# Chunked sliding-window attention without 28 tensor products whose results nobody reads

## What is computed

```python
def swa_sinks(h, cos, sin, w_in, b_in, sinks, w_out, b_out):
    proj = h @ w_in + b_in
    q = apply_rope(...)   # 16 heads of 64, in 4 groups of 4
    k = apply_rope(...)   # 4 key heads
    v = proj[..., qd + kd:]
    # chunks of 64 positions; a query chunk sees its own and the previous chunk
    scores = jnp.einsum("bnqhgd,bnkhd->bnhgqk", q, kb) * (SW_HEAD_DIM ** -0.5)
    scores = jnp.where(valid, scores, -jnp.inf)
    m = jnp.maximum(jnp.max(scores, axis=-1, keepdims=True), sink)
    pexp = jnp.exp(scores - m)
    probs = pexp / (jnp.sum(pexp, axis=-1, keepdims=True) + jnp.exp(sink - m))
    o = jnp.einsum("bnhgqk,bnkhd->bnqhgd", probs, vb)
    return o.reshape(b, s, qd) @ w_out + b_out
```

## Time and profile before

| | |
|---|---|
| time, median of 3 runs | 1420.49 us (1419.34 to 1420.56) |
| profiled execution: its time | 1417.11 us |
| profiled execution: span of the trace | 1415.4 us |
| PE busy | 1360.9 us (96%) |
| DVE busy | 791.6 us (56%) |
| ACT busy | 533.4 us (38%) |
| POOL busy | 252.4 us (18%) |
| granted TensorE clock, mean | 0.993 |

### The profile page before, as it was taken

One profiled execution on the slowest core, in us unless ns is written; L12 is line 12 of the kernel. 1 busy time (PEld: TensorE's weight loads), 2 busy tenths in 40 slices (PEclk: granted clock), 3 DMA queues, 4 the chain that ended last, 5 costly groups with the idle time before them and its releaser, 6 DMA issues.

```text
span 1415.4 us, 18106 instructions
## 1 busy us (share of the span) xinstructions
PE 1360.9 (96%) x6594; PEld 1120.3 (79%) x6594; DVE 791.6 (56%) x1205; ACT 533.4 (38%) x901; POOL 252.4 (18%) x243
## 2 busy tenths in 40 slices
PE   7899999999899999999999999989999999999998
PEld 5678878888778888888888878758888888888877
DVE  5557777777674343343456677674443434435655
ACT  6444445444154132231334431453332313223344
POOL 3654545453030000000002110002010000000211
PEclk9899999999999999999999999999999999999999
DMA  6233233222323223223322352503322232223221
GB/s 176 65 84 78 60 81 84 55 61 69 99 77 117 90 91 117 89 89 102 105 89 82 97 100 66 115 6 108 116 90 89 89 119 89 89 89 104 85 80 60
DMA packets 168575, 125.67 MB, mean 89 GB/s; under 512 B 35873, under 2 KB 165186, under 8 KB 168514
## 3 DMA queue, kind: packets, MB, share of 16 engines
q1 hardware_dynamic: 167410, 123.01, 29.2%
q10 hardware_dynamic: 1104, 1.84, 0.5%
HBM read 116.96 MB, written 5.25 MB: 86 GB/s over the span
## 4 chain that ended last, share of the span: by engine, by line
PE 75%; DVE 11%; ACT 3%; issue 3%; DMA 3%; DVEq 2%; POOL 2%; POOLq 0%; SPq 0%; ACTq 0%
PE psum L148 22%; PE psum L150 21%; PE psum L149 21%; DMA xScaled<-inv_blocks 2%; PE psum L890 2%; DVE wL L140 1%; PE psum L900 1%; ACT wH L132 1%; DMA inv_blocks<-blk 1%; DVE bL L1397 1%; DVE hT L1598 1%; DVEq L1168 1%; DVE terms L1166 1%; DVE acc L1596 1%; PE psum L1917 1%
## 5 line engine op out<-in xcount | busy, mean ns | idle before, releaser
L148 PE MATMUL psum<-aH,wH 128*128 128x512 f32 x896 | 361.2, 403 | 8.3 <-issue 5.4
L150 PE MATMUL psum<-aL,wH 128*128 128x512 f32 x896 | 351.3, 392 | 0.0
L149 PE MATMUL psum<-aH,wL 128*128 128x512 f32 x896 | 350.5, 391 | 0.0
L140 DVE TENSOR_TENSOR wL<-wRaw,wH 128x2048 fp32r<-128x2048 f32 (+2 forms) x125 | 241.0, 1933 | 128.5 <-ACT wH L132 122.9
L148 PE MATMUL psum<-bH,wH 128*128 128x512 f32 x720 | 284.8, 396 | 2.3 <-DVE pleT L2043 1.6
L150 PE MATMUL psum<-bL,wH 128*128 128x512 f32 x720 | 280.9, 390 | 0.0
L149 PE MATMUL psum<-bH,wL 128*128 128x512 f32 x720 | 280.8, 390 | 0.0
L132 ACT CAST wH<-wRaw 128x2048 fp32r<-128x2048 f32 (+2 forms) x109 | 196.9, 1813 | 219.9 <-PE psum L150 219.9
L148 PEld LDWEIGHTS psum<-aH,wH 128*128 128x128 f32 x896 | 169.4, 189 | 42.0 <-issue 6.8
L150 PEld LDWEIGHTS psum<-aL,wH 128*128 128x128 f32 x896 | 169.0, 189 | 36.2
L149 PEld LDWEIGHTS psum<-aH,wL 128*128 128x128 f32 x896 | 169.6, 189 | 32.1 <-issue 0.5
(11 more groups left out here) (295 smaller groups left out, 1498.6 us busy)
## 6 DMA issues: line engine op xcount, KB each, us to landing
wRaw<-in_mlp_w_up SPq DMA_DIRECT2D x64, 512.0 KB
wRaw<-in_mlp_w_down SPq DMA_DIRECT2D x64, 512.0 KB
wRaw<-in_dn_w_in SPq DMA_DIRECT2D x32, 512.0 KB
wRaw<-in_ple_w_gate SPq DMA_DIRECT2D x16, 512.0 KB
xScaled<-inv_blocks SPq DMA_DIRECT2D x16, 256.0 KB, 3.2
wRaw<-in_sw_w_in SPq DMA_DIRECT2D x16, 256.0 KB
wRaw<-in_sw_w_out SPq DMA_DIRECT2D x16, 256.0 KB
wRaw<-in_dn_w_out SPq DMA_DIRECT2D x8, 384.0 KB
```

The source lines that it names most:

```text
L140: last = [nc.vector.tensor_tensor(o, r, h_.bitcast(F32), ALU.subtract) for o, r, h_ in zip(*([v if half is None else v[:, half * v.shape[1 ...
L148: nc.tensor.matmul(o, wh, xh, start=first, stop=False)
L149: nc.tensor.matmul(o, wl, xh, start=False, stop=False)
L150: return nc.tensor.matmul(o, wh, xl, start=False, stop=last)
```

## The change

The definition of `keep_clock` and its two calls go. Nothing else is edited; the waits of every engine, the order of all other instructions and the transfers stay as they are.

```diff
-            def keep_clock(count):
-
-                for _ in range(count):
-                    nc.tensor.matmul(bank[7], wH[:, n % 2, 0:P], X[0][:, 0, :], start=True, stop=True)
-
...
             for i in range(3):
                 scores(i, [1])
-            keep_clock(8)
             for i in range(ATB):
                 t = i // KVH
                 if i + 3 < ATB:
                     scores(i + 3, [1] if i < 1 else range(2))
-                if i < KVH:
-                    keep_clock(5)
                 pe.wait_ge(pr_ok, i + 1)
```

## The result

The changed kernel is slower: 1426.61 us median (7 runs, 1422.23 to 1429.73) against 1419.34 us for the kernel before (7 runs, the three shown above among them, 1414.87 to 1420.56), a ratio of 1.0057 with a 95% interval of 1.0038 to 1.0075. Forecast were 1418.8 us, a range up to 1421.1, and "within 0.2%". The slowdown is what rival (a) describes, to which the prediction gave 0.07.

The account below looks back on a forecast made before the run. DVE was taken to set the pace from block 4 to 15. Its waits of 0.49 + 1.39 = 1.88 us, trimmed to 1.7 for a clock fall, came off the median: 1420.49 - 1.7 = 1418.8 us, range 1416.8 to 1421.1.

Parts of the forecast that it names:

- rival (a): In the opening the clock stays at 1.2 GHz and PE becomes the bound: 4.1 us slower, 1424.6 us; chance 0.07.
- the 7.5 us on the chain: Dense products on the chain of work in the opening, 2.04 us once and 1.36 us four times; only 1.88 us gainable.
- DVE's two waits: DVE's idle time for transposes ahead of its copies of blocks 1 and 3, 0.49 and 1.39 us, would both go.
- ACT did not take over: ACT, idle 2.47 us ahead of the copy of block 2, was checked as next to be late and forecast not to be.
- The gap: Idle time of PE ahead of block 0's transposes, from 895.21 to 897.98, forecast at 2.77 us.
- a fall once, around the new gap: Clock at 1.2 GHz once near block 0's transposes, for 3.4 us; gain 1.6 to 1.88 us, or 1.1 if 6.9 us.
- the prediction's own sign of being wrong: In the opening of the changed kernel's profile, the clock being down for over 7 us would show the forecast wrong.

Follow-up runs that it names:

- the fitted kernel: Against the kernel before: dense products cut to 2, 3, 3, 3 in turns 0 to 3, four added in turn 4, eight ahead of the loop kept; ratio 0.9994.
- the first experiment: Against the kernel before: only the eight dense products ahead of the loop stay, the twenty in the first four turns go; ratio 0.9998.
- the kernel with the tail filled: The kernel before with its 28 dense products and eight more, two in turn 13 and six in turn 14; ratio 0.9993.

## Why the prediction was wrong

**What bounds the kernel, and the sum at 2.4 GHz: right.** Of the 7.5 us on the chain only DVE's two waits were to be had, 0.49 + 1.39 = 1.88 us. With the clock held in the opening (23 products, fitted to the gaps) the attention shortened by 1.85 us, the copies had no idle time ahead, and ACT did not take over.

**The gap: right.** 2.95 us against 2.77, and the clock fell around it, as said.

**The step that failed** is the one behind it: "So I expect a fall once, around the new gap, and the upper clock soon after." Its length was put at 3.4 us, or 6.9 at worst. It was 47.8 us in the profile of the changed kernel and 34.1 us in its repeat, where the prediction's own sign of being wrong was "over 7 us". The step rested on two rows. One was the stretch from 910 to 944 us, in which the same blocks ran at 1.00 without dense products. That showed that this work keeps a clock that is already up. It was read as if it also brought it up soon. The runs show the difference: at 2.4 GHz the blocks ran on at 1.00 in every profile as long as no gap of 1 us or more came, and behind the opening's gap of 2.95 us, with no dense products to follow, the same blocks stayed at 1.2 GHz for 47.8, 34.1 and 30.7 us, with PE idle for under 1 us in 46 in the first of them. At 1.2 GHz a block takes PE 5 us and not 3, so "busy" shows PE full. The other row was the return within 3.4 us at 944 us, in transposes and value products without scores; the clock was back at 948.4, a microsecond ahead of the output product. It was taken for the opening's mix, which has 2 of its 5 us in scores.

**The price: right per block, wrong in how many blocks pay it.** Rival (a) put the end of block 3's transposes at 912.12 - 897.98 = 14.1 us behind the start of block 0's; it was 911.07 - 896.85 = 14.2 us behind. The estimate of twice the time for scores was right (2.07 us). Rival (a) then took one further block, 4.1 us slower in all; in the profile six more followed at 1.2 GHz, and the attention was 12.8 us slower. Wrong too was its weight of 0.07, which rested on the longest low stretch in the trace of before, 6.9 us. That trace has dense work throughout the opening and no fall there, so it can't show how long one lasts there. In all 17 runs of the changed kernel the time at 1.2 GHz was 45 us or more.

**The medians fit an estimate.** The changed kernel's runs have 56.6 - 22.8 = 34 us more at 1.2 GHz. What one such microsecond costs in this stage can be taken from three profiles without dense products in the loop, against the 55.99 us of the fitted kernel, which has 3.4 us at 1.2 GHz at its tail. The changed kernel has these too and 47.8 us more, the other two have none there and so 30.7 and 27.3 us more: (70.68 - 55.99) / 47.8 = 0.31, (64.39 - 55.99) / 30.7 = 0.27 and (63.23 - 55.99) / 27.3 = 0.27. That makes 9.0 to 10.4 us, less the 1.88 gained: 7.1 to 8.6 us, if all 34 us lie in the attention, and 7.3 were measured.

**A gap that the prediction did not see.** A quicker opening makes PE wait 1.41 us in place of 0.89 ahead of block 4. This came out only in the first experiment, and it may be why eight well-placed products alone gained nothing in the mean.

**The Trainium skill's rule** (TensorE: Matmul & The Clock Gate, section Why this matters for your kernels) was cited against the change and should have weighed more. It names idle gaps of some 3 us; at 2.95 us the clock fell in six profiles of six. Here it also fell at gaps of 1.05, 1.41, 1.60 and 1.95 us, though at 1.95 us only in half of the profiles, so the measured gaps decide.

**Open:** why two dense products in a row a turn don't bring the clock back and five do, and how much of it lies in the kind of work (scores are matmuls over 64 of the array's 128 rows, and the timelines show no more than how long they take). Why a fall behind the opening's gap lasted 30.7 us and more and one behind the gap ahead of block 4 6.8 to 13.6 us was not separated: the gap's length and its place both differ. Nor is it shown why the same gap costs the clock in one execution and not in the next. That holds outside the attention too: the clock fell behind the gap of 1.53 us at 46 us in the profile of before, and behind the one of 1.55 us there in that of the kernel with the tail filled it did not. Single runs of the kernel before, with 11 to 40 us at 1.2 GHz, differ by 5 us and more, and which gaps cost them the clock was not followed run by run.

## What to carry to other kernels

Work whose result nobody reads may be what keeps TensorE's clock up, so its price is not its own time but that of the work behind it for as long as that runs at half the clock. Before such work is taken out, look for the idle gap that it covers, and for the gaps that open elsewhere when the stage gets quicker. And ask two questions, not one: does the remaining work keep the clock, and would it bring it back soon. If such work costs time, cut it to what fits between the waits rather than away.

## What the runs showed of the chip

The level of the clock is not given by the work of the moment alone. The attention's work ran at 2.4 GHz with PE busy 27.5 of 34 us and at 1.2 GHz with PE busy 45.15 of 46 us, each without leaving its level. The Trainium skill (TensorE: Matmul & The Clock Gate, section HAM oscillation — how this bites in real kernels) tells of falls caused by waits; that a stream of matmuls with hardly a gap can stay down for 47.8 us stands beside it as measured here.

Behind five products of 128x512 in a row, 2.3 us at 1.2 GHz, the clock was back within 3 us in two profiles, and these two kernels spent 40 us a run at 1.2 GHz where the changed one spent 54 to 57. Six pairs did not bring it back in 37.5 us. How long the stay lasts varies within one kernel: 47.8 us in the first profile of the changed kernel, 34.1 in the second:

```profile
893.00:928.00 35.00, 32.05 (x106) 0.51 0.29 62
929.00:950.00 21.00, 16.70 (x96) 1.00 0.00 0
```
